# Splitting all gate units and moving part of the low-part subtraction to GpSimd in a two-block transformer kernel

## What is computed

```python
def hybrid_mixer(h, ...):
    (u_conv, q, kc, vc, ks, vs, kw, vw, g_nsa_heads, g_conv, g_attn) = jnp.split(
        h @ w_in, SPLIT_POINTS, axis=-1)
    conv_out = conv_module(u_conv, ...)
    nsa_out = nsa_attention(...)
    y = jax.nn.sigmoid(g_conv) * conv_out + jax.nn.sigmoid(g_attn) * nsa_out
    return y @ w_out

def conv_module(u, dw_w, dw_b, ln_g, ln_b, pw_w):
    a, gt = jnp.split(u, 2, axis=-1)
    v = a * jax.nn.sigmoid(gt)
    v = lax.conv_general_dilated(v, dw_w[:, None, :], ...) + dw_b
    v = jax.nn.silu(layer_norm(v, ln_g, ln_b))
    return v @ pw_w

def peer(xn, w_query, sub_keys, expert_u, expert_v):
        ...
        sc, ci = lax.top_k(cand, PEER_TOPK)
        g = jax.nn.softmax(sc, axis=-1)
        u = expert_u[e]
```

## Time and profile before

| | before |
|---|---|
| median of 3 runs (lowest, highest) | 1555.35 us (1553.8, 1555.42) |
| profiled execution, device time | 1557.67 us |
| its span, first to last instruction | 1555.2 us |
| mean granted clock of TensorE | 0.993 |
| instructions | 30922 |
| busy: PE / DVE / ACT / POOL | 1521.0 / 1150.7 / 811.9 / 270.3 us |
| moved by DMA | 257.78 MB, 166 GB/s |

### The profile page before, as it was taken

One profiled execution on the slowest core, in us unless ns is written; L12 is line 12 of the kernel. 1 busy time (PEld: TensorE's weight loads), 2 busy tenths in 40 slices (PEclk: granted clock), 3 DMA queues, 4 the chain that ended last, 5 costly groups with the idle time before them and its releaser, 6 DMA issues.

```text
span 1555.2 us, 30922 instructions
## 1 busy us (share of the span) xinstructions
PE 1521.0 (98%) x10782; PEld 1414.7 (91%) x10782; DVE 1150.7 (74%) x2427; ACT 811.9 (52%) x1456; POOL 270.3 (17%) x363
## 2 busy tenths in 40 slices
PE   7999998999999999999999989999999999999998
PEld 7998886999999998799999989999999888888886
DVE  5799899765666666867999975888888566666664
ACT  5546677654544446565555554333334554554454
POOL 2010331000100000000000004888886000000000
PEclk9999998999999999999999999999999999999999
DMA  7573333543465554433555555444444555555653
GB/s 251 189 248 130 126 113 109 163 163 133 165 202 179 186 178 147 163 111 110 174 189 178 175 168 175 142 135 138 146 136 158 193 191 195 192 191 191 198 190 108
DMA packets 70858, 257.78 MB, mean 166 GB/s; under 512 B 8272, under 2 KB 8480, under 8 KB 70528
## 3 DMA queue, kind: packets, MB, share of 16 engines
q1 hardware_dynamic: 67824, 246.97, 48.2%
q0 software_dynamic: 2960, 9.86, 2.0%
HBM read 254.67 MB, written 1.08 MB: 164 GB/s over the span
## 4 chain that ended last, share of the span: by engine, by line
PE 86%; DVE 8%; ACT 3%; issue 1%; DMA 1%; POOL 0%; SPq 0%; DVEq 0%; ACTq 0%
PE bank L368 17%; PE bank L369 17%; PE bank L370 17%; PE bank L992 7%; PE bank L990 7%; PE bank L991 7%; PE bank L969 4%; DVE ring_lo L1646 2%; PE bank L380 1%; DVE arena L1743 1%; PE bank L457 1%; DVE arena L1770 1%; ACT arena L1264 1%; ACT ring_hi L1120 1%; PE bank L535 1%
## 5 line engine op out<-in xcount | busy, mean ns | idle before, releaser
L1646 DVE TENSOR_TENSOR ring_lo<-ring_raw,ring_hi 128x1024 fp32r<-128x1024 f32 x459 | 562.7, 1230 | 175.1 <-ACT ring_hi L1120 172.4
L368 PE MATMUL bank<-operand_hi,ring_hi 128*128 128x256 f32 x2144 | 619.6, 289 | 15.2 <-DVE ring_lo L1705 7.4
L369 PE MATMUL bank<-operand_lo,ring_hi 128*128 128x256 f32 x2144 | 608.0, 284 | 0.0
L370 PE MATMUL bank<-operand_hi,ring_lo 128*128 128x256 f32 x2144 | 608.0, 284 | 0.0
L1120 ACT ACTIVATE ring_hi<-ring_raw 128x1024 fp32r<-128x1024 f32 x459 | 480.0, 1049 | 77.0 <-PE bank L370 64.3
L368 PEld LDWEIGHTS bank<-operand_hi,ring_hi 128*128 128x128 f32 x2144 | 412.5, 192 | 18.9 <-DVE ring_lo L1705 7.4
L369 PEld LDWEIGHTS bank<-operand_lo,ring_hi 128*128 128x128 f32 x2144 | 413.0, 193 | 0.3
L370 PEld LDWEIGHTS bank<-operand_hi,ring_lo 128*128 128x128 f32 x2144 | 412.5, 192 | 0.0
L1104 POOL TENSOR_SCALAR onehots<-iota_k,routeT 128x128 f32<-128x128 f32 x256 | 207.6, 826 | 235.2 <-ACT routeT L1568 198.8
L990 PE MATMUL bank<-ring_hi,hidden_hi 128*128 128x512 f32 x512 | 199.2, 389 | 0.0
L991 PE MATMUL bank<-ring_lo,hidden_hi 128*128 128x512 f32 x512 | 199.2, 389 | 0.0
(11 more groups left out here) (298 smaller groups left out, 1717.8 us busy)
## 6 DMA issues: line engine op xcount, KB each, us to landing
ring_raw<-in_stream SPq DMA_DIRECT2D x467, 512.0 KB, 3.5
arena<-bias_rows POOLq DMA_DIRECT2D x8, 384.0 KB, 3.9
arena<-in_memT SPq DMA_DIRECT2D x2, 512.0 KB, 5.0
arena<-in_xT POOLq DMA_DIRECT2D x1, 1024.0 KB, 7.4
arena<-in_w POOLq DMA_DIRECT2D x2, 512.0 KB, 10.5
arena<-in_memT POOLq DMA_DIRECT2D x1, 1024.0 KB, 5.2
out_rows<-arena SPq DMA_DIRECT2D x2, 512.0 KB, 2.6
arena<-arena POOLq DMA_DIRECT2D x4, 128.0 KB, 4.7
```

The source lines that it names most:

```text
L368: pe.matmul(out, wh, xh, start=start, stop=False, **kw)
L369: pe.matmul(out, wh, xl, start=False, stop=False, **kw)
L370: return pe.matmul(out, wl, xh, start=False, stop=stop, **kw)
L1646: dve.tensor_tensor(w_lo[:, slot, 0:n], raw[:, slot, 0:n], (raw if n == 1 else w_hi)[:, slot, 0:n].bitcast(F32), ALU.subtract)\
```

## The change

It has eight parts, in the order of the program.

1. The list WHOLE and `project_whole` go; all 16 gate units are split and go through `project_cols`. ACT always writes `w_hi`.
2. A list SHARED of 14 units comes in: `uconv` + 6, + 9, + 12, + 15, `q` + 3, `q` + 6, `ks` + 1, and `gattn` + 2 to + 14 in steps of two, the former whole units. For these POOL makes columns 256 to 1023 of the low part (`shared_lo`, 128x768) and signals `pool_lo`; DVE waits for that and makes the other 256 columns.
3. Where the unit whose low part has just been made is shared, DVE does six taps and not four, from `uconv` + 6 on. That is so in six iterations.
4. The first gate unit uses bank 0 and not bank 7 of PSUM.
5. ACT takes two and then four of the six exponentials of an even head, and not three and three, around the copy of a gate.
6. At the start ACT squares x in the second `xk` iteration and not the first, and DVE makes the low parts of units 3 and 4 before it waits for `onehot` and the constants.
7. The last normalisation of the first block moves from DVE to POOL, as 8 tensor_scalar and 8 tensor_tensor instructions; DVE waits for them before the second block's projection adds to x. ACT rounds units up to `q2` + 6 before it takes the root of a variance.
8. In the routing ACT takes the exponentials after 44 gelus, not 48, and DVE does the second half of the lookups before it waits for them.

```diff
-        WHOLE = [U["gattn"] + n for n in range(2, 16, 2)]
+        SHARED = [U["uconv"] + 6, U["uconv"] + 9, U["uconv"] + 12, U["uconv"] + 15, U["q"] + 3, U["q"] + 6, U["ks"] + 1] + [U["gattn"] + n for n in range(2, 16, 2)]
+        SHARE = 256
...
             def gate_slot(n):
-                if U["gattn"] + n in WHOLE:
-                    project_whole(U["gattn"] + n, 7, ("gate", n))
-                else:
-                    project_cols(U["gattn"] + n, 7, ("gate", n))
+                project_cols(U["gattn"] + n, 7 if n else 0, ("gate", n))
...
+            def shared_lo(u):
+
+                s, c = u % RING, slice(SHARE, D)
+                pool.wait_ge(hi_ready, u + 1)
+                pool.tensor_tensor(w_lo[:, s, c], raw[:, s, c], w_hi[:, s, c].bitcast(F32), ALU.subtract).then_inc(pool_lo, 1)
...
+            for u in SHARED[:4]:
+                shared_lo(u)
             for kv, (name, src) in enumerate((("kc", kcT), ("vc", vcT))):
...
+            for u in SHARED[4:7]:
+                shared_lo(u)
...
+                if s:
+                    for u in SHARED[7:9] if hh == 1 else SHARED[8 + hh // 2:9 + hh // 2]:
+                        shared_lo(u)
...
+            pool.wait_ge(rows_scale, 1)
+            for c in range(KC):
+                pool.tensor_scalar(xT[:, c, :], xT[:, c, :], cols[:, G_FINAL, c:c + 1], 1.0, ALU.mult, ALU.mult).then_inc(pool_seq, 1)
+            for c in range(KC):
+                pool.wait_ge(pool_seq, 3 + c)
+                pool.tensor_tensor(xT[:, c, :], xT[:, c, :], std[:], ALU.mult).then_inc(rows_scaled, 1)
...
-                if j == 0:
+                if j == 1:
                     act.wait_ge(x_in, 16)
...
-            with act.Fori(0, EARLY // RING - 4) as i:
+            with act.Fori(0, EARLY // RING - 5) as i:
...
             def lo(u, slot):
                 dve.wait_ge(hi_ready, u + 1)
-                n = 1 if isinstance(u, int) and u in WHOLE else D
-                dve.tensor_tensor(w_lo[:, slot, 0:n], raw[:, slot, 0:n], (raw if n == 1 else w_hi)[:, slot, 0:n].bitcast(F32), ALU.subtract)\
+                n = D
+                if isinstance(u, int) and u in SHARED:
+                    dve.wait_ge(pool_lo, SHARED.index(u) + 1)
+                    n = SHARE
+                dve.tensor_tensor(w_lo[:, slot, 0:n], raw[:, slot, 0:n], w_hi[:, slot, 0:n].bitcast(F32), ALU.subtract)\
                    .then_inc(lo_ready, 1)
...
-            lo_to(RING - 1)
+            lo_to(RING + 1)
             dve.wait_ge(onehot_in, 32)
...
-                    some_taps(4)
+                    some_taps(6 if u + RING - 1 in SHARED else 4)
...
-            rstd(("norm", N_2))
-            lo_to(U["q2"] + 3)
-            for c in range(KC):
-                if c == KC // 2:
-                    lo_to(U["q2"] + RING)
-                dve.scalar_tensor_tensor(xT[:, c, :], xT[:, c, :], cols[:, G_FINAL, c:c + 1], std[:], ALU.mult, ALU.mult)
+            emptied(dve, ("norm", N_2))
+            dve.reciprocal(std[:], std[:]).then_inc(rows_scale, 1)
             lo_to(U["q2"] + 1 + RING)
...
+            after(lookups(1))
+            early_lo(1)
             dve.wait_ge(c_exp, TT)
...
-            after(ins)
-            early_lo(1)
-            lookups(1).then_inc(routed, 1)
+            ins.then_inc(routed, 1)
```

More of the change, by code:

```diff
@@ L140, in build @@
         csum = at(25600, S)
-        whole = [at(10240, D), at(26624, D)]
         onehot = at(6144, 512)
@@ L373, in chunk_ready @@
                 pe.wait_ge(opnd_ready, READY[k] - KC + c + 1)
-            def project_whole(u, b, name):
-                unit(u)
-                take(b, name)
-                for c in range(KC):
-                    m = pe.matmul(bank[b][:, 0:S], whole[u // 2 % 2][:, c * P:(c + 1) * P], hf[:, c, :], start=c == 0, stop=c == KC - 1)
-                m.then_inc(unit_done, 1)
             def project_cols(u, b, name=None, first=None, last=False):
@@ L1118, in hi @@
                     act.wait_ge(unit_done, u - RING + 1)
-                dst = whole[u // 2 % 2] if isinstance(u, int) and u in WHOLE else w_hi[:, slot, :]
-                act.activation(dst, raw[:, slot, :], ACT.Copy).then_inc(hi_ready, 1)
+                act.activation(w_hi[:, slot, :], raw[:, slot, :], ACT.Copy).then_inc(hi_ready, 1)
             def hi_to(n):
@@ L1300, in _ @@
             for pair in range(NH // 2):
-                gate_copy(2 * pair)
+                gate_copy(2 * pair, 7 if pair else 0)
                 probs_out(2 * pair)
@@ L1306, in _ @@
                 if pair + 1 < NH // 2:
-                    nsa_exp(2 * pair + 2, range(3))
+                    nsa_exp(2 * pair + 2, range(2))
                 probs_out(2 * pair + 1)
@@ L1312, in _ @@
                 if pair + 1 < NH // 2:
-                    nsa_exp(2 * pair + 2, range(3, 6))
+                    nsa_exp(2 * pair + 2, range(2, 6))
                     nsa_exp(2 * pair + 3)
@@ L1562, in _ @@
                 act.activation(pick[:, 2, t, :], pick[:, 2, t, :], ACT.Exp, scale=rcol[:, t:t + 1]).then_inc(c_exp, 1)
-            with act.Fori(EARLY // RING - 4, EARLY // RING - 1) as i:
+            with act.Fori(EARLY // RING - 5, EARLY // RING - 1) as i:
                 for k in range(RING):
@@ L2061, in _ @@
             for t in range(TT):
-                lo_to(U["q2"] + 2 + t + RING)
+                if t:
+                    lo_to(U["q2"] + 3 + RING)
                 after(dve.tensor_scalar(va[:, t, :], va[:, t, :], stat[:, 2 * t:2 * t + 1], stat[:, 2 * t + 1:2 * t + 2],
```

9 lines of the change are left out of this document (5 added, 4 removed).

## The result

The change makes the kernel slower: 1561.24 us (median of 8, 1558.17 to 1562.68) against 1555.38 (median of 8, 1553.8 to 1558.04), a ratio of 1.0037 (95% interval 1.0028 to 1.0046), so 5.9 us where 5.7 less were forecast. So traces are used here for places, medians for totals.

A forecast was written before the change was run, and what follows sets the result against it. PE, busy 98% of the span, was taken as the bound. Start -2.0, middle +0.7 (DVE +2.2, clock -1.5), normalisation -0.5 and routing -3.9 sum to -5.7, so 1549.7 us from a median of 1555.35; range 1540.0 to 1558.0.

The forecast's parts named there:

- The start (-2.0): Part 6: PE's wait of 1.33 us near 20 us and the half clock behind it go; -2.0, range -2.9 to 0.
- PE's gate units: Part 1: splitting seven whole units saves PE 0.77 us each, 5.4 in all, collected only where PE is the bound.
- The holds: POOL's parts hold DVE: four beside taps 1.6 us each, +6.4; seven in the loop 0.6 each, +4.2.
- What idle time takes up: DVE's 10.9 us of idle time from 90 to 250 us absorb its added time; DVE ends +2.2 later.
- the sum of the middle: DVE's chain from 28 to 263 us, parts 1 to 3: savings, holds and late parts sum to +13.1 us on DVE.
- The late parts: DVE stands still until POOL is done: `uconv` + 9 +1.8, `q` + 3 +2.4, `gattn` + 2 +2.0, `uconv` + 6 0.
- The clock at `xv` (-1.5): A shorter wait before `xv` may avoid the half clock behind it, which costs 3.1 us; half taken, -1.5.
- the slower rival: Third of the rivals: POOL holds DVE in the loop for its whole instruction, 1.6 us a part; +6.0, 1561.4, chance 0.10.
- The normalisation (-0.5): Part 7: DVE loses 3.2 us of work to POOL, whose operations may hold it 4.2; -0.5, range -1.2 to +1.5.
- The routing (-3.9): Part 8: PE's waits of 3.18 and 0.40 us and one of 0.3 behind them go; -3.9.
- The first rival: POOL's parts cost DVE little: holds half as large, none late; middle -9.8, total -16.2, 1539.2, chance 0.20.
- The second (1554.4): DVE ends 3.7 us later and the clock still falls, the start gives 0.3 only; -1.0, 1554.4, chance 0.20.

The follow-up runs named there:

- e2: The kernel before with part 6 (the start) alone: 1555.00 us, ratio to before 0.9993.
- e4: The kernel before with parts 6 and 8 (start and routing), its seven gate units left whole: 1548.87 us, ratio to before 0.9951.
- e9: The changed kernel with no low part made on POOL and the last normalisation back on DVE: 1547.87 us, ratio to before 0.9950.
- e3: The changed kernel with no low part made on POOL, the taps at their new places: 1548.23 us, ratio to before 0.9947.
- e12: The changed kernel with POOL's part for `gattn` + 2 alone left out: 1554.97 us, ratio to before 0.9997.
- e1: The kernel before with part 8 (the routing) alone: 1549.92 us, ratio to before 0.9959.
- e7: The changed kernel with POOL's parts for the seven gate units only: 1552.60 us, ratio to before 0.9992.
- e5: The changed kernel with part 7 undone (last normalisation back on DVE): 1558.40 us, ratio to before 1.0026.
- e10: The changed kernel with POOL's part for `uconv` + 9 alone left out: 1558.37 us, ratio to before 1.0022.
- e11: The changed kernel with POOL's part for `q` + 3 alone left out: 1555.81 us, ratio to before 1.0006.
- e6: The changed kernel with POOL's parts for the seven units before the loop only: 1554.76 us, ratio to before 1.0000.
- e8: The changed kernel without POOL's parts for `uconv` + 6, `uconv` + 9, `q` + 3 and `gattn` + 2: 1551.13 us, ratio to before 0.9979.

## Why the prediction was wrong

**The start (-2.0): within its range, by no settled amount.** The first `uconv` copies came 1.7 us earlier in the pair of traces and the clock stayed at 1.00. e2 gives 1.1 +- 1.4. That the pair shows 1.7 is chance: at an early rise of PE's rate part 6 gives 2.8, at a late one 0.1 (see e2).

**PE's gate units: right that nothing is collected, too high in size.** A unit was to save 0.77 us, to be collected only where DVE isn't the bound. It saves 0.6. It isn't collected: e4 and e9 are equal.

**The holds: right.** Forecast 1.6 us for each part beside taps and 0.6 in the loop; measured 1.6 three times and 1.2 once, and in the loop 0.7 for five parts and 1.55 for one. POOL's part alone was to take 1.8 us and takes 1.83. DVE's busy time to `xv` was to change by -5.6 + 1.9 + 6.4 + 4.2 = +6.9 and did by +6.5. The number was right for a reason that was half wrong. I took the hold as a part of POOL's instruction, 0.53 us for 256 columns. The rows show it whole: DVE's instruction waits until POOL's has ended, and before it POOL's had waited for DVE's. The Trainium skill, "SBUF — State Buffer", section "SBUF: two separate sides", which states an exclusive lock for the whole instruction, was the better reading, and the trace agrees (a tap of 2.08 us ending 0.28 behind POOL, with 0.47 of its own work). The page names VectorE's operations with two inputs from SBUF and those in a two-port performance mode; here a tensor_scalar with one was held too, and no run shows in which mode it ran.

**What idle time takes up: the step that failed most.** I let 10.9 us of DVE's idle time absorb the sum of the middle ("with all of it used DVE ends +2.2 later"). DVE's idle time, in stretches that begin and end with the same instruction in each kernel (length less busy time in the views of stretches):

| up to the start of | before | e3 | after |
|---|---|---|---|
| the low part of `uconv` + 1, from 28 us | 3.49 | 0.75 | 1.81 |
| that of `uconv` + 8 | 5.91 | 5.91 | 6.70 |
| that of `uconv` + 13 | 2.35 | 2.35 | 4.35 |
| that of `q` + 4 | 0.14 | 0.14 | 3.55 |
| that of `gattn` + 3 | 6.99 | 1.17 | 3.51 |
| the first matmul of `xv` | 4.00 | 2.51 | 4.63 |

Each of the second to the fifth row has one late part in it, which adds 0.8, 2.0, 3.4 and 2.3 us. Apart from these the last three rows, which hold the 10.9 us of the forecast, fell from 11.1 to 5.9 us, so 5.2 us were taken up and not 10.9. Nearly all of it lay at one place, the first pair, where DVE had waited for PE's scores; before and then after:

```profile
DVE arena L1770 <- PE bank L539: 5.5, 4, 4.8
```

```profile
DVE arena L1781 <- PE bank L531: 2.1, 1, 2.1
```

Of the 5.9 us left, 3.8 are left in e3 as well. In its last stretch these are 48 short pauses between DVE's own operations that need each other's results, 2.5 us together and the same in before and after: more work on DVE doesn't fill them. The other 2.1 us are the second row: DVE waiting at 187.00 us for scores of a PE that was late by its own wait and half clock behind `gattn` + 2.

**The late parts: the second step that failed.** Forecast +1.8, +2.4 and +2.0, and 0 for `uconv` + 6, 6.2 in all; the waits grew by 2.0, 3.4, 2.3 and 0.8 us, 8.5 in all, and one more hold of 1.55 came at `gattn` + 2. (DVE's idle time before these four is 11.5 us, but at `uconv` + 9 it waits 2.28 us for the rounding in before too, and the wait behind `uconv` + 6 is 0.7 shorter.) Missed were that DVE would come to `q` + 3 at 102.65 and not 103.7; that POOL's two parts at head 1 run back to back, so the second holds the quarter for which the first was waited; and what is queued behind that quarter, the maxima of head 2, ACT's copies and PE, with a clock at half behind its 4.56 us of idleness. For this last the middle had no term, and e12, without that one part, has its `xv` 3.9 us earlier from the copy on.

So DVE ended 8.1 later and not 2.2 - 2.0 = 0.2: 5.7 by idle time not taken up, 2.3 by the waits, 0.3 by the start, less 0.4 of busy time.

**The clock at `xv` (-1.5): right**, -1.3; the wait there fell to 1.70 us, and a short stretch at half clock stayed. But the same kind of loss came back in the loop, which only the slower rival had, and there for another wait.

**The normalisation (-0.5): wrong sign**, +0.6 in the trace. POOL's operations took some 1.2 us each for 128x256 and not 0.75, and held DVE's low parts.

**The routing (-3.9): right, and more**: -4.9 in the traces, -6.4 (4.2 to 8.4) in e1. Where the 1.0 us beyond PE's three waits comes from wasn't looked into. In after the exponentials come 4.1 us earlier though PE is 7.5 late there, and PE has no wait (60.00 busy of 60.00 in the third row of the stretches of after):

```profile
904.46 1.28 ACT L1570 ACT_TABLE_LOAD   x1
```

These terms account for the 2.6 us between the spans of the two traces. The medians' 5.9 are 3.3 more, and the late `xv` in the trace of before (2.9 us, against that of e1) is about as much: it is the trace from which every term here was taken.

**The rivals.** The slower one (1561.4) has the right time and a wrong mechanism, so its hit is luck. It had POOL hold DVE for 1.6 us in each pair; the hold there is 0.7 in five pairs, the loop's period isn't longer than without POOL (13.1 against 13.2 us), and e7 puts the loop's cost at one place, the first pair. The loss is in the late parts, the holds before the loop and idle time that could not be used. My reason for giving it 0.10 (taps are few in a pair) was right about holds and said nothing of lateness. The first rival (holds of half the size, nothing late) fails on both counts. The second (1554.4) had the stretch at half clock that stayed at `xv`, but priced the unused idle time at 1.5 us where it was 5.7. The range ended at 1558.0 since the third rival was left out of it and the waits for POOL had no upper bounds of their own.

## What to carry to other kernels

Before an engine that is full is given a helper, take the helper's whole instruction as the hold of each operation of the full engine beside it that reads SBUF, and set it against what is saved; here a quarter kept (0.34 us) and three quarters given away cost 1.2 to 1.6 to save 0.8. The price of a helper is above all when it is done: for each piece write down when its input is ready, what the helper does before, and when the main engine arrives, and follow what is queued behind the wait on all engines. Count as cover only idle time that waits for another engine and will still be there when the work comes; here that was 5.2 of 10.9 us, and pauses between the engine's own dependent operations were none of it. And compare traces from an instruction behind the start on, if their starts differ.

## What the runs showed of the hardware that was not expected

- DVE and POOL took turns by whole instructions: POOL's 128x768 subtraction, 1.83 us alone or beside DVE's reads of PSUM, lasted 2.89 with a DVE subtraction ahead of it, and the tap behind it 2.08 rather than 0.47. It held a tensor_scalar of 128x6 elements (0.87 against 0.17 us) as well, in five pairs, but not the operations whose first input was in PSUM.
- DVE's busy time in a profile contains such holds. 219.32 us with help and 219.27 without it read alike, though the first kernel had given away three quarters of 14 subtractions.
- PE's clock was granted at half (1.2 and not 2.4 GHz) behind a wait of some 4.5 us in each of the five traces that had this wait (after, e5, e7, e10, e11; it lasted 7.4 to 8.8 us from the wait's end on), and in none of e3, e6, e8, e9 and e12, where the waits of that place were 1.4 us or less.
- Behind other waits the outcome differed between traces with the same wait: behind the 1.70 us before `xv` half clock followed in nine traces and not in e9; behind the 1.9 us at the first gate unit in before and e4 and not in e1 and e2; behind the 3.18 us in the routing in e2 and not in before.
- At the start PE's matmuls of 128x256 came 0.21 us apart and then 0.12, and the change between them fell anywhere from 10.5 to 13.7 us in the fourteen traces.
